# Differential attention in an encoder trunk: the key norms summed by a stationary of ones and inverted on all columns, in place of per-token sums turned back by TensorE

## The chip, the cores and the metric

The kernel runs on one core of one Trainium2 chip. The metric is the device time of one execution in microseconds (us), the median of several. The engines are named as the profile names them: PE (TensorE), DVE (VectorE), ACT (ScalarE), POOL (GpSimd) and SP (SyncE, which issues DMAs).

## The reference

A trunk of two layers over 16 + 512 and 16 + 256 tokens (800 in all), width 1024, all in fp32. Layer 0 mixes with a bidirectional mLSTM, layer 1 with differential attention, and each is followed by a SwiGLU feed-forward layer. The change touches only the attention of layer 1:

```python
def _rms_f32(x, g):
    xf = x.astype(jnp.float32)
    y = xf * lax.rsqrt(jnp.mean(xf * xf, axis=-1, keepdims=True) + RMS_EPS)
    return y * g.astype(jnp.float32)

    q = proj[..., :D_QK_W].reshape(B, L, D_HEADS, 2, D_HD)
    k = proj[..., D_QK_W:2 * D_QK_W].reshape(B, L, D_HEADS, 2, D_HD)
    v = proj[..., 2 * D_QK_W:].reshape(B, L, D_HEADS, 2 * D_HD).astype(jnp.float32)
    q = partial_rope(_rms_f32(q, g_q), cos, sin) * (D_HD ** -0.5)
    k = partial_rope(_rms_f32(k, g_k), cos, sin)
    ...
        s = jnp.einsum("bhcqd,bhckd->bhcqk", qblk, k)
        p = jax.nn.softmax(s, axis=-1)
        a = p[:, :, 0] - lam * p[:, :, 1]
        return jnp.einsum("bhqk,bhkv->bhqv", a, v)
    ...
    o = _rms_f32(o, g_sub) * (1.0 - lambda_init)
```

There are 8 heads, each with two components of 64 rows. Keys need one norm factor per token and component, queries likewise, and the output of each head one per token.

## The kernel before

**Layout.** Activations lie feature by token: a head's keys are one tile of 128 rows (two components of 64) by 800 tokens, its queries 128 by 768 (the 16 learned tokens of each sequence ask nothing). A projection block is 8 steps over the width, `run_block`; a step is 6 matmuls (high and low parts of a split fp32 product, two stretches of tokens). The finished block lies in PSUM banks 6 and 7 until DVE evacuates it (`evacuate`, `evacuate_inner`), and only then may PE open the next block there (`acc_free`).

**The schedule.** Every engine has its own program, written out by hand in one order, and they meet at semaphores. `head(hd, ...)` on each engine attends with head hd and, woven between, projects keys, queries and values of head hd + 1. Query tiles are numbered 0 to 5; tiles 0 to 3 see 528 keys, tiles 4 and 5 see 272. For each tile i: PE computes the scores (`attn_scores`), DVE takes the maxima (`maxima`), ACT the exponentials (`exps`), DVE joins the two components (`combine`), PE turns the result (`turn_attention`), ACT copies it (`turned`), PE multiplies by the values (`attend`), and DVE scales (`output`). Scores of 528 keys fill PSUM banks 0 to 3, so the scores of a tile wait for the exponentials of the tile before. The last scores in `head(hd)` are already those of head hd + 1, tile 0, and so need that head's normalised keys (`kn_ready`). Head 0 and the loop's six heads contain this hand-over, seven in all; head 7 has none.

**Key norms before.** ACT squares the keys (`k_sq`). PE sums them over 64 rows by eight small matmuls: the squares of 128 tokens are the stationary operand and two columns of ones and zeros the moving one (`square_sum`, line 1214), which leaves the sums with tokens on the partitions, 2 columns a tile. ACT takes the roots of all 28 columns (`key_query_roots`), DVE inverts 16 of them and spreads each over 64 columns (`invert_key_roots`), PE turns eight tiles of it back to feature by token (`turn_key_roots`, line 1244), in two parts, and DVE multiplies the keys by what PE left in PSUM (`normalise_k`), in two parts. Query norms stay with tokens on the partitions and are used as scales of the exponentials.

**Output norms before.** The output of head hd - 1 is finished in `head(hd)`: ACT takes roots (`output_roots`), DVE inverts 6 columns and scales six 128 by 128 tiles (`scale_output`, line 2105), PE turns them (`turn_output`, two parts), and ACT and DVE split them (`deliver`).

**Ahead of head 0** the same steps run for head 0's keys, and DVE's order there is: rope of keys and queries, key norms, query norms, then the evacuation of the values block, for which PE's next block waits.

## Time and profile before

| | |
|---|---|
| Time, median of 3 runs | 1863.31 us (1863.25 to 1863.38) |
| Span of the profiled execution | 1860.4 us |
| PE busy (matmuls) | 1849.7 us, 99% |
| DVE busy | 1235.1 us, 66% |
| ACT busy | 879.7 us, 47% |
| POOL busy | 1162.6 us, 62% |
| PE's share of the chain that ended last | 91% |
| Granted clock of PE | 9 (tenths, 9 or more) in all 40 slices |
| Attention layer, head 0 to head 7 | about 943 to 1320 us of the span |

The profiled execution is read by its span; the timed runs are 2.9 us longer than it, since they hold what lies around it. Busy time is the time in which an engine had an instruction under way; for PE the ends of matmuls are modelled and overlap the next, so the distance from start to start is the better price. In the timeline, rows of like instructions are merged, "x6" counting them; an fp32 matmul shows as two records. What stands in brackets is the idle time before the row and what ended it.

### The profile page before, as it was taken

Reading aid. Unit: us, or ns where it says so; the run is one execution under the profiler, and the core shown is the slowest. Engines: PE = TensorE matmul, PEld = TensorE weight load, DVE = VectorE, ACT = ScalarE, POOL = GpSimd, SP = SyncE. Lnnn points to the kernel's source line nnn. Section 1 sums busy time; section 2 is a strip of 40 time slices with the busy share of each in tenths; the row PEclk is TensorE's granted clock in tenths of the full one; section 3 lists DMA queues with packets and bytes.
Section 4 is the critical chain, followed back from the end, with each engine's and each line's share of the span. In section 5 each row is a group of like instructions: output and inputs, shape, how many; then the busy total and the mean of one; then the engine's idle time right before and its main releaser. Section 6 shows DMA issues by size and latency. Waiting matters only on the chain.

```text
span 1860.4 us, 31456 instructions
## 1 busy us (share of the span) xinstructions
PE 1849.7 (99%) x10845; PEld 1742.0 (94%) x10845; DVE 1235.1 (66%) x2072; ACT 879.7 (47%) x1855; POOL 1162.6 (62%) x1533
## 2 busy tenths in 40 slices
PE   9999999999999999999999999999999999999999
PEld 8888889999999999999988888888889999999998
DVE  6756566768576757576876666666587575756663
ACT  6444343455444445454444444444465454444553
POOL 4453644468687878788843333333558788887885
PEclk9999999999999999999999999999999999999999
DMA  8789997549697977774475666664233535353534
GB/s 270 257 240 237 222 259 173 183 108 228 209 237 238 235 227 218 250 232 118 107 145 121 126 124 124 130 118 91 74 90 110 148 99 157 100 153 101 154 112 133
DMA packets 380153, 309.51 MB, mean 166 GB/s; under 512 B 14395, under 2 KB 322398, under 8 KB 379766
## 3 DMA queue, kind: packets, MB, share of 16 engines
q1 hardware_dynamic: 349472, 237.81, 42.1%
q0 software_dynamic: 28416, 69.21, 20.5%
q8 instruction: 73, 1.20, 0.3%
q10 hardware_dynamic: 2134, 0.82, 0.2%
q14 instruction: 58, 0.48, 0.1%
HBM read 302.16 MB, written 144.04 MB: 240 GB/s over the span
## 4 chain that ended last, share of the span: by engine, by line
PE 91%; DVE 5%; ACT 1%; issue 1%; DMA 1%; POOL 0%; SPq 0%; ACTq 0%; DVEq 0%; POOLq 0%
PE ps L974 51%; PE ps L884 26%; PE ps L1155 3%; PE ps L1312 3%; PE ps L1280 2%; PE ps L1302 1%; PE ps L1130 1%; PE ps L1214 1%; DVE rstd L1502 1%; PE ps L1164 1%; DVE sx L1554 0%; PE ps L1244 0%; DVE mx L2077 0%; DVE gt L1661 0%; DMA wk<-in_x_prompt_dram 0%
## 5 line engine op out<-in xcount | busy, mean ns | idle before, releaser
L974 PE MATMUL ps<-sx,wh 128*128 128x400 f32 (+1 forms) x2044 | 530.3, 340 | 0.9 <-POOL wl L808 0.5
L808 POOL TENSOR_TENSOR wl<-raw,wh 128x256 fp32r<-128x256 f32 (+1 forms) x432 | 355.6, 855 | 97.9 <-ACT wh L2243 96.4
L774 POOL CAST wh<-raw 128x256 fp32r<-128x256 f32 x248 | 102.5, 456 | 450.6 <-PE ps L884 424.9
L974 PEld LDWEIGHTS ps<-sx,wh 128*128 128x128 f32 x2044 | 373.4, 188 | 3.0 <-ACT gt_first L2258 0.9
L974 PE MATMUL ps<-sx,wl 128*128 128x400 f32 (+1 forms) x1022 | 347.6, 340 | 0.0
L808 POOL TENSOR_TENSOR wl<-raws,wh 128x256 fp32r<-128x256 f32 x328 | 283.8, 910 | 84.4 <-ACT wh L2243 84.0
L1715 DVE TENSOR_TENSOR h<-h,ps 128x400 f32<-128x400 f32 (+1 forms) x280 | 154.5, 559 | 131.5 <-PE ps L974 131.4
L974 PE MATMUL ps<-fx,wh 128*128 128x400 f32 (+1 forms) x904 | 235.3, 341 | 0.1
L884 PE MATMUL ps<-xh,wh 128*128 128x512 f32 (+1 forms) x752 | 211.2, 357 | 0.0
L884 PE MATMUL ps<-xl,wh 128*128 128x512 f32 (+1 forms) x752 | 207.3, 349 | 0.0
L778 POOL TENSOR_TENSOR wl<-raw,wh 128x256 fp32r<-128x256 f32 x248 | 198.8, 831 | 5.1
L884 PE MATMUL ps<-xh,wl 128*128 128x512 f32 (+1 forms) x752 | 201.3, 345 | 0.0
L2243 ACT ACTIVATE wh<-raw 128x512 fp32r<-128x512 f32 (+2 forms) x268 | 142.7, 535 | 106.5 <-PE ps L974 92.3
L974 PEld LDWEIGHTS ps<-sx,wl 128*128 128x128 f32 x1022 | 191.9, 188 | 0.0
L2243 ACT ACTIVATE wh<-raws 128x512 fp32r<-128x512 f32 (+2 forms) x202 | 108.5, 538 | 159.0 <-PE ps L974 150.5
L974 PEld LDWEIGHTS ps<-fx,wh 128*128 128x128 f32 x904 | 164.6, 188 | 0.5 <-issue 0.5
L974 PE MATMUL ps<-fx,wl 128*128 128x400 f32 (+1 forms) x452 | 153.7, 340 | 0.0
L974 PE MATMUL ps<-sx,w5h 128*128 128x400 f32 (+1 forms) x532 | 138.3, 341 | 0.3 <-ACT gt L2258 0.3
L884 PEld LDWEIGHTS ps<-xl,wh 128*128 128x128 f32 x752 | 126.2, 188 | 10.2
L884 PEld LDWEIGHTS ps<-xh,wl 128*128 128x128 f32 x752 | 124.5, 188 | 10.8
L884 PEld LDWEIGHTS ps<-xh,wh 128*128 128x128 f32 x752 | 120.6, 189 | 14.5 <-issue 3.8
L808 POOL TENSOR_TENSOR w5l<-raw,w5h 128x256 fp32r<-128x256 f32 x112 | 94.8, 868 | 22.5 <-ACT w5h L2243 22.1
(330 smaller groups left out, 3552.0 us busy)
## 6 DMA issues: line engine op xcount, KB each, us to landing
in_sums<-in_ffn_w_in_dram SPq DMA_DIRECT2D x16, 1536.0 KB, 10.7
raw<-in_sums SPq DMA_DIRECT2D x96, 256.0 KB, 3.0
in_sums<-in_ffn_w_in_dram SPq DMA_DIRECT2D x16, 1280.0 KB, 7.2
raw<-in_ffn_w_in_dram SPq DMA_DIRECT2D x80, 256.0 KB, 3.0
raws<-in_sums SPq DMA_DIRECT2D x80, 256.0 KB, 3.1
raw<-out_sums SPq DMA_DIRECT2D x120, 128.0 KB, 2.6
raws<-in_ffn_w_in_dram SPq DMA_DIRECT2D x52, 256.0 KB, 3.1
raw<-in_m_w_in_dram SPq DMA_DIRECT2D x24, 512.0 KB, 4.8
```

Source lines behind the costliest of these rows:

```text
L774: ins = pool.tensor_copy(wh[:, slot, c], raw[:, slot, c])
L778: ins = pool.tensor_tensor(wl[:, slot, c], raw[:, slot, c], wh[:, slot, c].bitcast(F32), ALU.subtract)
L808: ins = pool.tensor_tensor(slot_of(n, 1)[:, c], raw_of(n)[:, c], slot_of(n, 0)[:, c].bitcast(F32), ALU.subtract)
L884: mm = pe.matmul(out, w[:, slot, k * P:(k + 1) * P], x[:, k, a:b], start=(k + q == 0), stop=(k == k_tiles - 1 and q == 2), skip_group_chec ...
L974: mm = pe.matmul(product_bank(layer, s, j), slot_of(n, low_w)[:, k * P:(k + 1) * P], x, start=(j in OPENS and k + q == 0), stop=(k == tile ...
L1130: mm = pe.matmul(flat(2)[0:tz, base + a:base + a + columns], k[:, 1, t0:t0 + tz], q[:, 0, START[s] + a:START[s] + a + columns], start=(t = ...
L1155: mm = pe.matmul(ps[0:tz, state_bank(i) + d, 0:M_DV + 2], w, v, start=(j == js[0] and t == 0), stop=(j == js[-1] and t == len(passes) - 1) ...
L1164: mm = pe.transpose(flat(2)[:, c * 1024 + t0:c * 1024 + t0 + tz], hn(i)[0:tz, c * P:(c + 1) * P], ident[0:tz, 0:tz])
L1280: return pe.matmul(both[:, c, a:b], wk[rows, odd, i * P:(i + 1) * P], wk[rows, 2 + odd, START[s] + a:START[s] + b], start=True, stop=True)
L1312: mm = pe.matmul(acc_o, at[:, i % 2, q, :], va[:, odd, j, :], start=(q == 0), stop=(j == js[-1]), skip_group_check=True)
L1715: ve.tensor_tensor(part, part, product_bank(layer, s, j), ALU.add if result_of(s, j)[0] >= 4 else ALU.subtract).then_inc(out_read, 1)
L2243: sc.activation(slot_of(n, 0)[:, 0:columns], raw_of(n)[:, 0:columns], ACT.Copy).then_inc(prod_hi, 1)
```

## The change

Key squares are summed by two matmuls whose stationary operand is a 128 by 128 matrix with two 64 by 64 blocks of ones (`blocks`), and whose moving operand is the 800 columns of squares, 512 and 288. The sums then lie feature by token already, each repeated over the 64 rows of its component. ACT takes the roots of all 800 columns, DVE inverts all 800 in SBUF, and multiplies the keys by them in one instruction. `turn_key_roots` and the spreading copy are gone. The scaling of the outputs goes to ACT, with the reciprocal left on DVE (the last two heads keep it on DVE). On PE the scores of the next head's tile 0 and the first part of `turn_output` move behind step 5 of the values block and `attend(4)`; one step earlier a wait for `o_ready` moves from `turn_attention` to `attend` for tiles 4 and 5. Ahead of head 0, its first scores move behind the first step of head 1's keys block.

```diff
             def key_sums(g, k, done=None):
...
-                keys = [lambda i=i: square_sum(i) for i in range(NQ, NQ + NT)]
-                return {k: [squares] + keys[0:4], k + 1: keys[4:]}
+                    pe.matmul(bank[:, 0:K_PART], blocks, k_sq[:, 0:K_PART], start=True, stop=True, skip_group_check=True)
+
+                def second():
+                    pe.matmul(ps[:, 0, 0:T - K_PART], blocks, k_sq[:, K_PART:T], start=True, stop=True,
+                              skip_group_check=True).then_inc(ks_done, 1)
+
+                return {k: [first], k + 1: [second]}
...
                 if first:
-                    keys_block(0, 3)
+                    keys_block(0, 1)
+                    attn_scores(0, 0, 0, first=True)
+                    keys_block(1, 3)
...
                 attend(hd, odd, 3)
-                if not last:
-                    turn_key_roots(hd + 1, 0)
-                beside(values_block, 3, 4, (2, 4, 5))
-                if not last:
-                    turn_key_roots(hd + 1, 1)
-                beside(values_block, 4, 5, (2, 5, 6))
+                beside(values_block, 3, 5, (2, 4, 6))
                 turn_attention(hd, 4, first)
 
-                if not last:
-                    attn_scores(hd + 1, even, 0)
-                if not first:
+                if last:
                     turn_output(hd - 1, even, 0)
                 beside(values_block, 5, 6, (3, 0, 3))
                 attend(hd, odd, 4)
+                if not last:
+                    attn_scores(hd + 1, even, 0)
+                    if not first:
+                        turn_output(hd - 1, even, 0)
+                    values_block(6, 8)
                 if not first:
                     turn_output(hd - 1, even, 1)
...
+            def invert_output_roots(hd):
+                ve.wait_ge(oroot, hd + 1)
+                ve.reciprocal(rs[:, 0:NQ], rs[:, 0:NQ]).then_inc(rs_ready, 1)
+
+            def invert_key_roots(g, part):
                 ve.wait_ge(qk_root, g + 1)
-                v(ve.reciprocal(qkr[:, odd, 2 * NQ:], qk2[:, 2 * NQ:]))
-                v.wait()
-                ve.tensor_copy(key_roots.rearrange("p (i f) -> p i f", i=2 * NT),
-                               qkr[:, odd, 2 * NQ:].unsqueeze(2).to_broadcast([P, 2 * NT, D_HD])).then_inc(lt_ready, 1)
+                columns = (slice(0, K_PART), slice(K_PART, T))[part]
+                v(ve.reciprocal(k_sq[:, columns], k_sq[:, columns]))
...
+            def normalise_k(g, odd, x):
                 v.wait()
-                v(ve.tensor_tensor(kd[rows, odd, at_col], bank[rows, keys.start - a:keys.stop - a], x[rows, keys], ALU.mult))
+                for rows, keys, at_col in ((slice(D_HD, P), slice(0, TAIL), slice(TAIL, 2 * TAIL)),
+                                           (slice(0, D_HD), slice(512, LENS[0]), slice(0, TAIL))):
+                    v(ve.tensor_tensor(kd[rows, odd, at_col], k_sq[rows, keys], x[rows, keys], ALU.mult))
                 v.wait()
-                ve.tensor_tensor(x[:, a:b], bank[:, 0:b - a], x[:, a:b], ALU.mult)\
-                  .then_inc((kn_part, kn_ready)[part], 1)
+                ve.tensor_tensor(x, k_sq, x, ALU.mult).then_inc(kn_ready, 1)
...
                 maxima(hd, odd, 5)
                 if not last:
-                    normalise_k(hd + 1, even, kx, 0)
+                    if not first:
+                        invert_output_roots(hd - 1)
+                    invert_key_roots(hd + 1, 0)
                 output(hd, odd, 3)
-                if not last:
-                    invert_query_roots(hd + 1, even)
-                    normalise_k(hd + 1, even, kx, 1)
-                if not first:
+                if last:
                     scale_output(hd - 1, even)
-
-                if last:
                     add_tile(OUT1 + 2, EARLY[2], 3)
                 else:
+                    invert_key_roots(hd + 1, 1)
+                    normalise_k(hd + 1, even, kx)
+                    invert_query_roots(hd + 1, even)
                     maxima(hd + 1, even, 0)
...
             def key_query_roots(g, bank=turn_bank):
                 sc.wait_ge(ks_done, g + 1)
                 sc.activation(k_sq[:, 0:K_PART], bank[:, 0:K_PART], ACT.Sqrt, bias=epsc, scale=1.0 / D_HD)
                 sc.wait_ge(qks_done, g + 1)
...
+                sc.activation(k_sq[:, K_PART:T], ps[:, 0, 0:T - K_PART], ACT.Sqrt, bias=epsc, scale=1.0 / D_HD)
+                sc.activation(qk2[:, :], square_sums, ACT.Sqrt, bias=epsc, scale=1.0 / D_HD).then_inc(qk_root, 1)
...
+            def scale_output(hd, odd):
+
+                sc.wait_ge(rs_ready, hd + 1)
+                sc.wait_ge(o_ready, hd * NQ + NQ)
+                for i in range(NQ):
+                    ins = sc.activation(on(odd, i), on(odd, i), ACT.Copy, scale=rs[:, i:i + 1])
+                ins.then_inc(os_ready, 1)
```

DVE's program at the end of a head in the loop, from the join of tile 4 (the first row) to the maxima of the next head's tile 0. Before (`spare` is the spread key roots, `ps` what PE turned, `wk` the keys):

```order
L2091 SCALAR_TENSOR_TENSOR wk<-wk,ratio 128x272
L2049 REGISTER_ALU
L2050 RECIPROCAL qkr<-qk 128x16
L251 REGISTER_ALU
L2052 COPY spare<-qkr 128x1024
L2076 REGISTER_ALU
L2077 TENSOR_REDUCE mx<-ps 128x2
L251 REGISTER_ALU
L2079 SCALAR_TENSOR_TENSOR nb<-mx,qkr 128x2
L2070 TENSOR_TENSOR kd<-ps,wk 64x16
L251 REGISTER_ALU
L2072 TENSOR_TENSOR wk<-ps,wk 128x512
```

In the changed kernel the same place, from the maxima of tile 5 on, where `spare` is now the squares, then the roots, then the inverted roots of all 800 columns:

```order
L2070 TENSOR_REDUCE mx<-ps 128x2
L251 REGISTER_ALU
L2072 SCALAR_TENSOR_TENSOR nb<-mx,qkr 128x2
L2046 RECIPROCAL rs<-rs 128x6
L2049 REGISTER_ALU
L2051 RECIPROCAL spare<-spare 128x512
L2089 TENSOR_SCALAR wk<-ps,rsum 128x128
L2051 RECIPROCAL spare<-spare 128x288
L251 REGISTER_ALU
L2064 TENSOR_TENSOR kd<-spare,wk 64x16 x2
L251 REGISTER_ALU
L2066 TENSOR_TENSOR wk<-spare,wk 128x800
```

The reciprocal of 16 columns and the copy stood ahead of the maxima of tile 5; two reciprocals of 512 and 288 columns stand behind it, and all of the keys' multiplication behind those.

PE's program in the same stretch before, from the second part of the turned key roots (L1244): a step of the values block (L884), tile 4 turned (L1302), the next head's tile 0 scores (L1285, L1280), the output turned (L1265):

```order
L1244 MATMUL ps<-cst,spare 128x16 x2
L884 MATMUL ps<-xh,wh 128x400 x2
L884 MATMUL ps<-xl,wh 128x400 x2
L884 MATMUL ps<-xh,wl 128x400 x2
L1298 REGISTER_ALU
L1302 MATMUL ps<-cst,wk 128x128 x2
L1302 MATMUL ps<-cst,wk 16x128
L1275 REGISTER_ALU
L1285 MATMUL ps<-kd,wk 128x2x16
L1280 MATMUL ps<-wk 128x512 x2
L1265 MATMUL ps<-cst,wk 128x128 x4
```

In the changed kernel, from tile 4 turned (L1294) on, `attend` being L1306 and the scores L1277 and L1272:

```order
L1294 MATMUL ps<-cst,wk 128x128 x2
L1294 MATMUL ps<-cst,wk 16x128
L886 MATMUL ps<-xh,wh 128x400 x2
L886 MATMUL ps<-xl,wh 128x400 x2
L886 MATMUL ps<-xh,wl 128x400 x2
L1306 MATMUL ps<-va,at 128x128 x3
L1265 REGISTER_ALU
L1267 REGISTER_ALU
L1277 MATMUL ps<-kd,wk 128x2x16
L1272 MATMUL ps<-wk 128x512 x2
L1257 MATMUL ps<-cst,wk 128x128 x4
```

One step of the block and the attend of tile 4 now stand ahead of the scores, and behind them only the last two steps of the block.

DVE's program ahead of head 0, before, from the end of the queries' rope to the evacuation of the values block (L1478), which PE's next keys block waits for:

```order
L2046 TENSOR_TENSOR wk<-wk,spare 128x768
L2050 RECIPROCAL qkr<-qk 128x16
L2052 COPY spare<-qkr 128x1024
L2070 TENSOR_TENSOR kd<-ps,wk 64x16
L2072 TENSOR_TENSOR wk<-ps,wk 128x512
L2070 TENSOR_TENSOR kd<-ps,wk 64x16
L2072 TENSOR_TENSOR wk<-ps,wk 128x288
L2057 RECIPROCAL qkr<-qk 128x12
L2059 TENSOR_SCALAR qkr<-qkr 128x12
L1478 TENSOR_TENSOR spare<-ps,rstd 128x800
```

And in the changed kernel:

```order
L2042 TENSOR_TENSOR wk<-wk,spare 128x768
L2051 RECIPROCAL spare<-spare 128x512
L2051 RECIPROCAL spare<-spare 128x288
L2064 TENSOR_TENSOR kd<-spare,wk 64x16 x2
L2066 TENSOR_TENSOR wk<-spare,wk 128x800
L2055 RECIPROCAL qkr<-qk 128x12
L2057 TENSOR_SCALAR qkr<-qkr 128x12
L1471 TENSOR_TENSOR spare<-ps,rstd 128x800
```

The order of the three jobs is the same; the first has other instructions, and the evacuation stands behind all of them.

## Rows read from the trace of the kernel before

**Rows 1.** One head by engine: length, busy times, granted clock, DMA share, GB/s

```profile
...
1077.90:1126.30 48.40, 48.30 (x306) 41.52 (x306) 32.45 (x72) 22.12 (x60) 17.26 (x27) 1.00 0.60 119
```

**Rows 2.** PE timeline, head's end into the next: start, us, line, tiles, count

```profile
...
1120.94 0.66 PE L1244 MATMUL ps<-cst,spare 128*128 128x128 f32 x4
...
1124.83 0.31 PE L1285 MATMUL ps<-kd,wk 128*128 128x32 f32 x2
...
1126.12 0.66 PE L1265 MATMUL ps<-cst,wk 128*128 128x128 f32 x4
...
1127.71 0.83 PE L1312 MATMUL ps<-va,at 128*128 128x128 f32 x6
...
1128.85 0.61 PE L884 MATMUL ps<-xh,wh 128*128 128x400 f32 x2
...
1131.45 0.31 PE L1285 MATMUL ps<-kd,wk 128*128 128x32 f32 x2
...
1132.75 0.94 PE L1312 MATMUL ps<-va,at 128*128 128x128 f32 x6
1133.44 0.61 PE L884 MATMUL ps<-xh,wh 128*128 128x400 f32 x2
...
1135.71 0.60 PE L1255 MATMUL ps<-cst,spare 128*128 128x128 f32 x4
```

**Rows 3.** DVE timeline beside it; in brackets idle before, releaser

```profile
...
1119.92 0.24 DVE L2050 RECIPROCAL qkr<-qk 128x16 f32<-128x16 f32 x1
...
1120.81 0.71 DVE L2077 TENSOR_REDUCE mx<-ps 128x2 f32<-128x544 f32 x1
...
1121.75 0.18 DVE L2070 TENSOR_TENSOR kd<-ps,wk 64x16 f32<-64x16 f32 x1
...
1122.57 0.34 DVE L2096 TENSOR_SCALAR wk<-ps,rsum 128x128 f32<-128x128 f32 x1
...
1126.24 1.26 DVE L2077 TENSOR_REDUCE mx<-ps 128x2 f32<-128x1056 f32 x1 [0.70 <-PE ps L1280]
...
1128.96 0.50 DVE L2091 SCALAR_TENSOR_TENSOR wk<-wk,ratio 128x272 f32<-128x272 f32 x1
...
1131.33 0.99 DVE L1478 TENSOR_TENSOR spare<-ps,rstd 128x800 f32<-128x800 f32 x1 [0.16 <-PE ps L884]
```

**Rows 4.** PE timeline earlier in that head

```profile
...
1097.74 0.59 PE L884 MATMUL ps<-xh,wh 128*128 128x512 f32 x2
...
1099.91 0.71 PE L1302 MATMUL ps<-cst,wk 128*128 128x128 f32 x5
...
1107.64 0.60 PE L884 MATMUL ps<-xh,wh 128*128 128x512 f32 x2
...
1111.82 0.73 PE L1280 MATMUL ps<-wk 64*128 64x272 f32 x4
```

**Rows 5.** PE timeline ahead of the attention layer: f32 matmuls with ones

```profile
...
914.41 1.50 PE L899 MATMUL ps<-wk,ones 128*128 128x400 f32 x4
...
916.10 0.52 PE L884 MATMUL ps<-xl,wh 128*128 128x512 f32 x2
```

**Rows 6.** One line, reciprocal of 800 columns: ns min, median, max

```profile
...
L1502 DVE RECIPROCAL rstd<-rstd x3: 5142/5153/5153, 413.6 to 1383.1; 128x800 f32<-128x800 f32 x3
```

**Rows 7.** Timeline of ACT beside it

```profile
...
1118.07 0.60 ACT L2665 ACTIVATE at<-ps 128x512 f32<-128x512 f32 x1 [0.23 <-PE ps L1302]
```

**Rows 8.** Timeline of DVE ahead of the first head

```profile
...
934.48 0.25 DVE L2050 RECIPROCAL qkr<-qk 128x16 f32<-128x16 f32 x1
...
938.04 0.99 DVE L1478 TENSOR_TENSOR spare<-ps,rstd 128x800 f32<-128x800 f32 x1
```

**Rows 9.** Timeline of PE at the same place

```profile
...
935.51 1.09 PE L1244 MATMUL ps<-cst,spare 128*128 128x128 f32 x8 [0.27 <-DVE spare L2052]
...
937.74 0.40 PE L1285 MATMUL ps<-kd,wk 128*128 128x32 f32 x2
...
942.81 0.41 PE L1285 MATMUL ps<-kd,wk 128*128 128x32 f32 x2
```

More of the change, by code:

```diff
@@ L83 @@
 A_PER = 72
-ATTN_SET = 9
+ATTN_SET = 11
 NPROD = 7
@@ L467, in trunk @@
         X_COLUMN = (0, 1, 2, 3, 5, 6, 4)
-        key_roots = spare[:, 0, 6:8, :].rearrange("p a b -> p (a b)")[:, 0:NT * P]
         PROBS = 4 * T
@@ L1219, in key_sums, with first @@
             def key_sums(g, k, done=None):
-                def squares():
+                bank = ps[:, 1, :] if done is None else turn_bank
+                def first():
                     pe.wait_ge(qsq_ready, g * 2 + 1)
@@ L1294, in turn_attention @@
             def turn_attention(hd, i, first):
-                if not (first and i == 0):
+                if i < 4 and not (first and i == 0):
                     pe.wait_ge(o_ready, hd * NQ + i)
@@ L2022, in _ @@
             ffn(0)
-            ve.memset(qk2[:, :], 1.0).then_inc(attn_set, 1)
+            ve.memset(blocks, 0.0).then_inc(attn_set, 1)
+            ve.wait_ge(attn_set, ATTN_SET - 2)
+            for rows in (slice(0, D_HD), slice(D_HD, P)):
+                ve.memset(blocks[rows, rows], 1.0).then_inc(attn_set, 1)
             ve.wait_ge(attn_set, ATTN_SET)
@@ L2055, in invert_query_roots @@
             def invert_query_roots(g, odd):
                 ve.wait_ge(qk_root, g + 1)
-                v(ve.reciprocal(qkr[:, odd, 0:2 * NQ], qk2[:, 0:2 * NQ]))
+                v(ve.reciprocal(qkr[:, odd, :], qk2[:, :]))
                 v.wait()
-                v(ve.tensor_scalar(qkr[:, odd, 0:2 * NQ], qkr[:, odd, 0:2 * NQ], D_HD ** -0.5, None, ALU.mult))
+                v(ve.tensor_scalar(qkr[:, odd, :], qkr[:, odd, :], D_HD ** -0.5, None, ALU.mult))
                 v.wait()
-            def normalise_k(g, odd, x, part, bank=turn_bank):
-                a, b = ((0, TILES[4][1]), (TILES[4][1], T))[part]
-                rows, keys, at_col = ((slice(D_HD, P), slice(0, TAIL), slice(TAIL, 2 * TAIL)),
-                                      (slice(0, D_HD), slice(512, LENS[0]), slice(0, TAIL)))[part]
-                ve.wait_ge(lt_turned, g * 2 + (part + 1))
+            def normalise_k(g, odd, x):
@@ L2193, in _ @@
             rope_end(0, qx, 0)
-            invert_key_roots(0, 0)
-            normalise_k(0, 0, kx, 0)
-            normalise_k(0, 0, kx, 1, second_bank)
+            for part in range(2):
+                invert_key_roots(0, part)
+            normalise_k(0, 0, kx)
             invert_query_roots(0, 0)
@@ L2715, in head @@
                 exps(hd, odd, 5)
+                turned(hd, 4)
                 squared(hd, odd, 3)
-                turned(hd, 4)
+                if not first and not last:
+                    scale_output(hd - 1, even)
                 if not first:
```

59 lines of the change are left out of this document (20 added, 39 removed).

## The prediction, made before the changed kernel ran

> **What bounds the kernel now.** I read the page first: PE is busy for 1849.7 of 1860.4 us and makes up 91% of the chain that ended last, so only what shortens PE's program, or makes it wait, moves the time. Then the stretches: in one attention head PE is busy for 48.30 of 48.40 us at a full granted clock, DVE for 32.45 [rows 1]. A busy engine whose ends are modelled can hide small waits, so I went to the timelines of PE and DVE at the end of a head. That stretch is one head, 48.4 us; the next one's own scores begin at 1131.45 [rows 2]. The reader is to see there that PE runs without a gap, and that DVE, though idle for a third of the head, is not idle at its end: from 1119.92 to the maxima at 1126.24 it has 0.70 us of idle time [rows 3]. The next head's scores start at 1124.83 [rows 2], and need keys that DVE finishes between 1122.57 and then. That hand-over is what the change rebuilds.
>
> **What PE is spared.** Two steps of a queries block take 1099.91 - 1097.74 = 2.17 us; the two that carry the eight key sums take 1111.82 - 1107.64 = 4.18 [rows 4]. The sums cost 2.01. Their successors are full fp32 matmuls of 800 columns. The nearest row is the same shape, ones as the stationary operand, 800 columns in four records: to 1.69 us from its start the block behind has also run a pair that costs 2.17 / 6 = 0.36, so it costs 1.33 [rows 5]. Spared: 0.68. The eight transposes go: 1120.94 to 1124.83 is 3.89 us [rows 2] and becomes two steps of 400 + 400 columns, 1135.71 - 1133.44 = 2.27, and the turning of tile 4. That turning is what 1128.85 to 1131.45 holds beside two steps: 2.60 - 2.27 = 0.33 [rows 2]. So 3.89 becomes 2.60, spared 1.29, waits included. Together 1.97 us a head, in seven heads.
>
> **What the keys now wait for.** DVE's work up to 1119.92 follows the queries block and is continuous, so it too comes 0.68 earlier: 1119.24. In a row behind it, with prices start to start: maxima of tile 5, 1121.75 - 1120.81 = 0.94 [rows 3]; reciprocal of 6 columns, 0.2 (that of 16 has 0.24 [rows 3]); two reciprocals; output 3, 0.34 less 0.08 of overlap = 0.26 [rows 3]; two small products of 0.18 with gaps, 0.4 [rows 3]; the product of 800 columns, 0.99 (evacuations of 800 columns are two-input instructions of the same size [rows 3, 8]). The reciprocal of 800 columns takes 5.15 us [rows 6], 21 times the 0.24 of 16 columns: (5.15 - 0.24) / 784 = 6.3 ns a column. Hence 512 columns take 3.35 and 288 take 1.95, with overlap 5.25 together. Sum: 0.94 + 0.2 + 5.25 + 0.26 + 0.4 + 0.99 = 8.04, keys ready at 1127.3.
>
> The Trainium skill ("VectorE: DVE Perf Modes", First, the fixed hardware budget) says that the reciprocal is an iterative divide with a repeat count of 8. Taken as 8 cycles a column at the page's 0.96 GHz that would be, as an estimate, 6.7 us for 800 columns; the trace has 5.15, and the measurement decides. By the page each hand-over would be 1.4 us later still.
>
> **When PE asks for them.** Before at 1124.83. Now 1.97 earlier, but with one step (1.14) and attend 4 (1133.44 - 1132.75 = 0.69 [rows 2]) moved ahead: 1124.69. So PE waits 1127.33 - 1124.69 = 2.6 us, and the scores start 2.50 later than before, although 1.97 of PE's work is gone and 1.83 was moved out of their way.
>
> **What is late next.** All that DVE does behind the maxima of tile 0 moves by 2.5 us too. PE behind the scores: 1.29 for them (1126.12 - 1124.83), 0.45 for the first outputs turned (1.59 to 1127.71 less a step), two steps 2.27, second part 0.2: it asks for the join of tile 5 at 1131.54. DVE ended that join at 1129.46 [rows 3]; 2.5 later, less 0.15 of idle time that closes, is 1131.8. Wait 0.3, then 0.33: the next head starts at 1132.19, 0.74 later than 1131.45. The evacuation of the values ended at 1132.32 [rows 3] and now ends between 1134.2 and 1134.8; PE asks for the bank at 1133.44 + 0.74 = 1134.18. That is a wait of 0 to 0.7, I take 0.35; and 0.1 (0 to 0.3) for ACT's copy of the values, which hangs on the same chain. A head becomes 0.74 + 0.35 + 0.1 = **1.2 us longer**, seven times 8.4 (0.7 to 1.6 a head: 5 to 11).
>
> **ACT.** Two roots of 512 and 288 columns come ahead of the copy for attend 3. ACT starts that copy, itself a read of 512 columns of PSUM, at 1118.07 after 0.23 of waiting, and it takes 0.60 [rows 7]. At 0.60 each at most, the roots add 1.2, less 0.68: the copy is up to 0.5 late. Attend 3 has five tiles, 1.15 at the rate of attend 4, so it began at about 1120.94 - 1.15 = 1119.8 [rows 2] and had some 0.9 to spare. So no wait; if a root costs double, 0.3 a head. The six scalings moved to ACT begin behind output 3, at about 1124.4, and at 0.6 each at most end by 1128.0, before PE turns them at 1127.3 + 1.3. On DVE they stood behind the keys and ahead of an idle 0.70 [rows 3]: nothing is won there.
>
> **Ahead of head 0** nothing covers the reciprocals. DVE's rope ends at 934.48 [rows 8]; three small clears in place of one, 0.25 (0.1 to 0.4). Then 5.25 + 0.4 + 0.95 (0.99 less overlap), and query norms, two instructions of 12 columns, 0.45: the evacuation starts at 941.8 in place of 938.04 [rows 8] and ends at 942.8. Only then may PE open the keys block; one step 1.14, and the first scores start at 943.95 in place of 937.74 [rows 9]. From there to the second scores exponentials decide (942.81 - 937.74 = 5.07 [rows 9], PE's own work 1.29 + 2.27 = 3.6), before as after, so **6.2 us** (5.5 to 6.7) pass to the end. PE idles for some 7 us in there, where it now has 0.27 [rows 9].
>
> The granted clock is 1.00 throughout [rows 1], and no row has PE idle for microseconds and busy behind it. Below, the clock stays: 0. Above, it falls to the lower level, 1.2 of 2.4 GHz, and the step and the scores on the path (1.14 + 1.29) take twice as long: 2.4, and 3.2 with the two steps that follow, 4.5 then against 3.8 of exponentials. I take 1.2, as no row decides.
>
> The Trainium skill ("TensorE: Matmul & The Clock Gate", What's actually happening) says that the clock falls to its lower level when PE has been idle and rises after sustained work. By that rule the term is 2.4 to 3.2 and the time 1.2 to 2 us above mine; by the rows alone it could be 0.
>
> **Sum** against the profile's own 1860.4: 6.2 + 8.4 + 1.2 = 15.8, that is 1876.2 as a span, and with the 2.9 around it 1879.1 against the median of 1863.3. I say 1879.
>
> **Rivals.**
> (1) *PE is spared and nothing waits.* DVE's reciprocals would have to be hidden. Then seven times -1.97, and ahead of head 0 -0.68 and -1.36 for the transposes and their wait [rows 9]: 1847.5. For it: DVE is idle for a third of a head, and 0.24 us for 16 columns looks cheap. Against it: [rows 6]. Each us off the pair of reciprocals takes 1 us off every one of eight places, so the sign turns where the pair costs 14.6 / 8 = 1.8 us less, 3.4 in place of 5.25. Chance 0.05.
> (2) *A draw*, within 0.2%, which is 3.7 us and about what a measurement tells: the same with the pair at 3.0 to 3.9, or with only the wait ahead of head 0 and hand-overs that break even: 1863 to 1867. Chance 0.04.
> (3) *The clock falls at every hand-over*, not only ahead of head 0. The scores and what follows them, 1.3 to 3 us, would take twice as long in seven heads: 9 to 21 more, 1888 to 1900. Against it: waits of 2.6 us only. Chance 0.06.
> (4) *The waits are smaller, and a loss stays*: some instruction of the DVE chain overlaps more than I count, 0.5 to 1 us a head: 1868 to 1874. Chance 0.15.
> (5) *My forecast*, 1874 to 1884: 0.70.
> Range 1868 to 1887. Faster 0.05, same 0.04, slower 0.91.
>
> **What the changed profile would show.** Reciprocals of 512 and 288 columns at 3.35 and 1.95 us; at each of seven scores of tile 0 PE idle for about 2.6 us, released by DVE's product of 800 columns; heads 49.6 apart in place of 48.4; an idle stretch of 7 us ahead of head 0, released by DVE's evacuation; no L1244; the pair of steps with key sums at 3.5 in place of 4.18; the clock just behind 942.8 shows which end of its term holds. The feed-forward stretches must be unchanged. I am wrong if reciprocals in place on the squares run at another rate than in place on the root of the norm, or if PE's idle time is not in front of these scores.

## The result: slower, and by more than predicted

The changed kernel takes 1890.85 us (median of 4 runs, 1888.74 to 1891.48) against 1863.28 (1862.69 to 1863.38): 1.0146 times, 95% interval 1.0133 to 1.016. That is 27.6 us slower; the prediction had 15.8, and its range ended at 1887. The profiled execution of after took 1891.11 us, its span 1889.1.

**The profile after.** The page, from the busy times and from the chain that ended last; before, PE made up 91% of the chain and DVE 5%:

```profile
PE 1849.7 (98%) x10685; PEld 1733.3 (92%) x10685; DVE 1263.0 (67%) x2030; ACT 894.8 (47%) x1899; POOL 1160.0 (61%) x1533
...
PE 81%; DVE 11%; issue 4%; ACT 3%; DMA 1%; POOL 0%; DVEq 0%; SPq 0%; ACTq 0%; POOLq 0%
```

PE is "busy" for as long as before, although it does less. These are the waits of PE from 930 to 1310 us (total, times, longest), in a program for which the same list held two waits before, of 0.3 and 0.2 us:

```profile
PE ps L1277 <- DVE wk L2066: 15.3, 7, 2.4
PE ps L886 <- DVE spare L1471: 7.4, 2, 7.2
PE ps L1247 <- ACT va L2650: 2.4, 4, 0.8
PE ps L1294 <- DVE wk L2084: 0.9, 3, 0.3
```

The first row is the forecast wait for the keys: six times 2.2 to 2.4 us, and 1.45 in the last. DVE's chain ahead of it, in the head of 1196 us:

```profile
1189.20 3.31 DVE L2051 RECIPROCAL spare<-spare 128x512 f32<-128x512 f32 x1
...
1192.60 1.94 DVE L2051 RECIPROCAL spare<-spare 128x288 f32<-128x288 f32 x1
...
1194.98 0.99 DVE L2066 TENSOR_TENSOR wk<-spare,wk 128x800 f32<-128x800 f32 x1
...
1197.62 1.26 DVE L2070 TENSOR_REDUCE mx<-ps 128x2 f32<-128x1056 f32 x1 [1.30 <-PE ps L1272]
```

3.31 and 1.94 us against 3.35 and 1.95 predicted. Now PE at two such places, one head apart:

```profile
1143.93 0.40 PE L1277 MATMUL ps<-kd,wk 128*128 128x32 f32 x2 [2.33 <-DVE wk L2066]
1144.26 2.08 PE L1272 MATMUL ps<-wk 64*128 64x512 f32 x4
1146.27 1.11 PE L1257 MATMUL ps<-cst,wk 128*128 128x128 f32 x4
...
1196.11 0.40 PE L1277 MATMUL ps<-kd,wk 128*128 128x32 f32 x2 [2.32 <-DVE wk L2066]
1196.44 1.13 PE L1272 MATMUL ps<-wk 64*128 64x512 f32 x4
```

The waits are equal, 2.33 and 2.32 us. Behind the first the scores take 2.08 us, behind the second 1.13. The busy times by stretch say why; the number behind POOL's is the granted clock:

```profile
1141.60:1143.93 2.33, 0.01 (x1) 0.01 (x1) 2.23 (x5) 1.10 (x4) 0.00 (x0) 1.00 0.58 109
1143.93:1145.00 1.07, 1.07 (x4) 0.80 (x6) 0.18 (x2) 0.00 (x0) 0.00 (x0) 0.65 0.00 0
1145.00:1146.00 1.00, 1.00 (x4) 0.00 (x0) 0.00 (x0) 0.00 (x0) 0.00 (x0) 0.50 0.00 0
...
1148.00:1150.00 2.00, 1.98 (x12) 1.70 (x10) 1.38 (x4) 1.83 (x5) 0.04 (x1) 1.00 0.00 0
...
1196.11:1198.11 2.00, 2.00 (x11) 1.20 (x12) 0.67 (x2) 0.00 (x0) 0.00 (x0) 1.00 0.20 37
```

The clock falls to 0.50, the lower of its two levels (1.2 of 2.4 GHz), at four of the seven hand-overs (1041, 1092, 1144 and 1247 us). At the first three it falls once PE works again, for some 3 us. At the fourth it is already down while PE still waits, and stays down for some 7 us (busy times by stretch again):

```profile
1244.40:1246.20 1.80, 0.00 (x1) 0.00 (x0) 1.70 (x4) 1.12 (x4) 0.00 (x0) 1.00 0.95 172
1246.20:1247.00 0.80, 0.24 (x2) 0.24 (x2) 0.74 (x3) 0.00 (x0) 0.00 (x0) 0.78 0.24 44
1247.00:1253.00 6.00, 6.00 (x19) 4.41 (x20) 2.74 (x6) 2.24 (x5) 0.00 (x0) 0.50 0.03 5
```

That head is the longest, 53.0 us. Ahead of head 0 the clock falls too, 2.6 us after PE's wait began:

```profile
936.31 0.53 PE L886 MATMUL ps<-xh,wl 128*128 128x400 f32 x2
944.06 1.03 PE L886 MATMUL ps<-xh,wh 128*128 128x400 f32 x2 [7.23 <-DVE spare L1471]
...
946.23 0.47 PE L1277 MATMUL ps<-kd,wk 128*128 128x32 f32 x2
946.62 2.08 PE L1272 MATMUL ps<-wk 64*128 64x512 f32 x4
...
951.95 0.41 PE L1277 MATMUL ps<-kd,wk 128*128 128x32 f32 x2 [0.40 <-ACT wk L2659]
```

PE is idle for 7.2 us as forecast; the step behind it takes 2.17 us (1.21 at the same place before) and the scores 2.40 (1.38).

**Where the time is.** The second scores of head 0 start at 951.95 (942.81 before [rows 9]); DVE's long reciprocal of rstd ahead of all this already starts 1.1 us later, so 8.0 belong to the change. From there to the start of the last head's own scores (a head's own scores are those of tile 1, the first in its program) pass 352.0 us, 333.5 before: 18.5. Middle heads are 50.8 to 53.0 us long, before 48.4 [rows 1]. The two profiled spans, 1889.1 and 1860.4, are 28.7 us apart; the 2.2 us that are left lie ahead of and behind the attention, where the change has nothing.

### The profile page after: what moved, and what is told of

Its sections match the earlier page's. It is cut to its first block, busy times and chain, and to the rows that moved or that the text cites. A ratio compares the mean times of both kernels' runs of the same rounds, so it can differ in the third digit from the quotient of the medians.

```text
span 1889.1 us, 31124 instructions
## 1 busy us (share of the span) xinstructions
PE 1849.7 (98%) x10685; PEld 1733.3 (92%) x10685; DVE 1263.0 (67%) x2030; ACT 894.8 (47%) x1899; POOL 1160.0 (61%) x1533
## 4 chain that ended last, share of the span: by engine, by line
PE 81%; DVE 11%; issue 4%; ACT 3%; DMA 1%; POOL 0%; DVEq 0%; SPq 0%; ACTq 0%; POOLq 0%
PE ps L976 50%; PE ps L886 21%; PE ps L1157 3%; PE ps L1272 2%; PE ps L1306 1%; DVE spare L2051 1%; DVE mx L2070 1%; PE ps L1132 1%; DVE rstd L1495 1%; PE ps L1294 1%; DVE spare L2033 1%; PE ps L1166 1%; ACT wk L2659 1%; DVE spare L2030 0%; DVE wk L2040 0%
## 5 line engine op out<-in xcount | busy, mean ns | idle before, releaser
L886 PE MATMUL ps<-xh,wh 128*128 128x512 f32 (+1 forms) x752 | 219.0, 366 | 7.7 <-DVE spare L1471 7.4
```

The lines of the kernel that those rows point to most:

```text
L886: mm = pe.matmul(out, w[:, slot, k * P:(k + 1) * P], x[:, k, a:b], start=(k + q == 0), stop=(k == k_tiles - 1 and q == 2), skip_group_chec ...
```

## Experiments

Two questions: is the clock the whole of the missing 12 us, and why does a head lose more than the wait explains? Shown edits are against after unless said otherwise. The kernel before, timed again beside each group of them, had medians of 1862.5 to 1863.0 us.

### PE's idle time filled

```diff
                 attend(hd, odd, 4)
                 if not last:
+                    pe.wait_ge(qk_root, hd + 2)
+                    for _ in range(12):
+                        pe.matmul(turn_bank[:, 0:HT], wh[:, even, 0:P], xh[:, 0, 0:HT], start=True, stop=True, ...)
                     attn_scores(hd + 1, even, 0)
...
             run_block(MIX1 + 2, 0, 3, k0=7)
+            for _ in range(30):
+                pe.matmul(turn_bank[:, 0:P], blocks, ident, start=True, stop=True, ...)
```

> After, with PE's seven waits at the hand-overs filled: twelve spare matmuls of 400 columns into a bank that nobody reads then, about 2.2 us at full clock, stand behind attend 4 and ahead of the next head's first scores. Nothing that the output needs is changed. Theory A (the part of the loss that was not forecast is TensorE's clock, which falls behind the idle time): the granted clock stays at 1.00 behind all seven hand-overs, the scores' row of 64x512 takes 1.13 us in each, the second scores of the heads stand 49.5 to 49.8 us apart rather than 50.8 to 53.0, and the time is 1881 to 1884 us; the 8.45 us ahead of head 0 stay. Rival B (the scores are slowed by something else that runs then, such as VectorE's reciprocals or ScalarE's scalings in the neighbouring banks): the time stays at 1890 us and the rows keep 1.7 to 2.1 us. Rival C (fillers delay the scores more than they save): over 1891.

Measured with the first part alone: 1885.24 us (1884.72 to 1885.75), ratio to before 1.0122 (1.0105 to 1.0139). All seven scores take 1.13 us at a granted clock of 1.00; the PE timeline of one:

```profile
1088.88 2.43 PE L1389 MATMUL ps<-xh,wh 128*128 128x400 f32 x12
1091.46 0.40 PE L1277 MATMUL ps<-kd,wk 128*128 128x32 f32 x2
1091.79 1.13 PE L1272 MATMUL ps<-wk 64*128 64x512 f32 x4
```

> The kernel with filled hand-overs, and thirty more spare matmuls of 128 fp32 columns (6.4 us at full clock) in PE's idle time of 7.2 us ahead of head 0. Theory A: the keys block and the first scores behind it run at a granted clock of 1.00, 1.14 and 1.38 us rather than 2.17 and 2.40, so the second scores start some 2 us earlier: 2 us less than with the hand-overs alone, 1879 to 1882 us, which is the forecast without its clock term. Rival B: no difference to the run with the hand-overs alone. Rival C: the fillers start at a lowered clock, take twice as long and push the keys block out: 2 to 5 us more.

Measured with both: 1883.15 us (1883.02 to 1883.46). The keys block behind the idle time is at full clock again:

```profile
935.81 6.86 PE L1420 MATMUL ps<-cst 128*128 128x128 f32 x60
943.22 0.64 PE L886 MATMUL ps<-xh,wh 128*128 128x400 f32 x2 [0.55 <-DVE spare L1477]
```

**What follows.** A is right in its mechanism and B falls: spare work alone, with no wait shortened, gives back 5.6 and 2.1 us. The clock costs 7.7 us in all, where the forecast had 1.2. But both times lie 1.2 us above A's bands, and middle heads are still 49.8 to 50.8 us long, not the 49.5 to 49.8 that I expected: from the second scores of head 0 to the last head's own pass 347.4 us, 13.9 more than before, where the forecast had 8.4. These 5.5 us are not the clock.

> After, with six spare matmuls ahead of each hand-over's first scores in place of twelve: 1.1 us of the 2.3 us wait are filled at its start, PE is idle for about 1.2 us behind them. Theory A (short idle times are harmless, as the 1.29 us in the run with the inversion hidden): the clock stays up at all seven, 1884 to 1886 us as with twelve. Rival B (any idle time near the scores can bring it down, by chance): the clock falls at one to three hand-overs, 1886 to 1890 us.

Six fillers in place of twelve: 1885.20 us (1884.66 to 1885.73), no fall at any hand-over, with PE idle for 1.1 to 1.3 us ahead of six of them (0.35 in the last). A holds.

### The order of PE's tail undone

Scores of tile 0 and the first turned outputs ahead of the sixth step and attend 4, as before.

> After, with PE's tail in the order of before: the next head's first scores and the first turned outputs stand ahead of the sixth step of the values block and of attend 4 again. Theory A: the keys come at the same time, PE asks 1.8 us earlier and waits 4.1 to 4.5 us in each head, then has 1.8 us more to do behind the scores; with 0.6 of other waits closed that is 1.0 to 1.4 us more in a head, 7 to 10 us, and the clock falls at all seven hand-overs, some 1 to 2 us at three more: 1898 to 1905 us. Rival B (the order makes no difference, since VectorE's chain ends last either way): 1889 to 1892.

Measured: 1900.37 us (1899.65 to 1900.85). PE's waits, 930 to 1310 us:

```profile
PE ps L1277 <- DVE wk L2062: 27.7, 7, 4.1
```

3.9 to 4.1 us each (3.2 in the last), and behind each of the seven the clock falls. As A: given DVE's chain, the new order is right, and worth 9.5 us.

### The inversion left out

```diff
-                v(ve.reciprocal(k_sq[:, columns], k_sq[:, columns]))
+                v(ve.tensor_scalar(k_sq[:, columns], k_sq[:, columns], 1.0, None, ALU.mult))
```

> After, with the two reciprocals of the key roots replaced by multiplications by 1.0 of the same columns in the same place: the inversion of the keys' roots is left out, all waits and orders stand. Theory A (the reciprocals' 5.25 us on VectorE make PE wait, and the wait brings the clock down): a multiplication of 512 columns takes 0.3 to 0.6 us, the pair about 1, so the keys are ready 4.2 us earlier, before PE asks; no wait at the hand-overs, clock 1.00 in all of them, PE's idle time ahead of head 0 at 3 us, and the time is 1848 to 1853 us, faster than before by 0.6 to 0.8%. Rival B (the new order of PE's tail or ScalarE's added work costs time of itself): 1863 us or more, with waits at other places.

Measured: 1862.84 us (1861.59 to 1863.82), ratio 1.0002 (0.9992 to 1.0011). **A falls; B holds** within the noise: it had 1863 or more, with waits at other places. No wait for the keys is left, and the 28 us are gone, but a middle head is 48.0 to 48.2 us long where 46.4 should do. Ahead of head 0 PE still waits 2.27 us, the clock falls there in this profile, and the second scores come 3.0 us later than before. The timelines of DVE, ACT and PE behind the scores of tile 0, which start at 1078.06:

```profile
1079.47 1.26 DVE L2070 TENSOR_REDUCE mx<-ps 128x2 f32<-128x1056 f32 x1 [3.15 <-PE ps L1272]
...
1082.18 0.50 DVE L2084 SCALAR_TENSOR_TENSOR wk<-wk,ratio 128x272 f32<-128x272 f32 x1
...
1082.74 0.55 PE L1294 MATMUL ps<-cst,wk 128*128 128x128 f32 x3 [0.33 <-DVE wk L2084]
...
1090.68 0.59 ACT L2650 ACTIVATE va<-ps 128x512 f32<-128x512 f32 x1
...
1091.32 0.66 PE L1247 MATMUL ps<-cst,spare 128*128 128x128 f32 x4 [0.83 <-ACT va L2650]
```

Read down: DVE's maxima wait for the scores; the join of tile 5 (L2084) stands behind them on DVE and ends 4.62 us after the scores began; PE, which now has only 4.2 us of work behind the scores, waits. What DVE does next (values evacuated, tile 0 joined, maxima of tile 1) is late by the same, ACT's exponentials and then its copy of the values (L2650) behind them. Before, that copy was ready 1.0 us ahead of the matmuls that turn it, the second L1255 of the head whose own scores start at 1131.45 [rows 2]:

```profile
1136.72 0.59 ACT L2650 ACTIVATE va<-ps 128x512 f32<-128x512 f32 x1
...
1138.33 0.60 PE L1255 MATMUL ps<-cst,spare 128*128 128x128 f32 x4
```

It began 5.27 us after the head's own scores; here it is 7.42 (1090.68 against 1083.26), 2.15 more. Laid beside before from own scores to own scores, the gaps are 0.56 at the join, 0.17 at the values' bank, 0.95 at the second half of the turned values: 1.7 us a head. The same three stand in the kernel with all idle time filled. None of it needs the reciprocals; it needs scores of tile 0 that stand 5.2 us ahead of the head's own, 6.6 before [rows 2].

### The same, with the old order, and then with VectorE's scaling

> The kernel without the inversion (multiplications by 1.0 in place of the two reciprocals; the inversion of the keys' roots is left out), with PE's tail back in the order of before: first scores ahead of the sixth step of the values block and of attend 4. The last run left 14 us unexplained: without the reciprocals PE never waits for the keys, yet a head is 48.06 us long and not 46.4. Theory A (the new place of the first scores costs it: they stand 5.2 us ahead of the head's own scores in place of 6.6, and VectorE's maxima, the join of tile 5, the evacuation of the values and ScalarE's copy behind them all hang on those scores; gaps of 0.56, 0.17 and 0.99 us follow): with the old order the gaps close, a head takes 46.4 to 46.7 us, and the time is 1850 to 1854 us. Rival B (ScalarE's two wide roots and six scalings, which stay, are what makes the copies late): a head stays at 48.0, the time at 1861 to 1864.

Measured: 1861.67 us (1860.6 to 1863.65), middle heads of 48.03 to 48.09. A named the right gaps, they are gone, and the time is not. B has the time and, in the scalings, the cause, though not by way of the copies. ACT's and PE's timelines:

```profile
1122.96 1.84 ACT L2639 ACTIVATE wk<-wk,rs 128x128 f32<-128x128 f32 x6
...
1124.86 0.66 PE L1257 MATMUL ps<-cst,wk 128*128 128x128 f32 x4 [1.46 <-ACT wk L2639]
```

The scaling that the change gave to ScalarE ends 2.8 us after the scores began at 1122.04, and in the old order PE wants to turn the scaled outputs 1.3 us after the scores began. So it goes back to VectorE:

```diff
                     invert_query_roots(hd + 1, even)
+                    if not first:
+                        scale_output(hd - 1, even)
                     maxima(hd + 1, even, 0)
```

> The kernel without the inversion and with the old order of PE's tail, and now with the scaling of the outputs back on VectorE, behind the keys and ahead of the next maxima, as before the change (the inversion of the keys' roots is left out). The run with ScalarE's scalings showed that the order alone gives nothing: the gaps at the join, the values' bank and the values' copy were gone, but PE waited 1.5 us in each of six heads for ScalarE's scaling when it came to turn the outputs, and a head stayed at 48.0 us. Theory A (the two things that the change did to PE's tail belong together: ScalarE's scalings end 2.8 us after the old place of the scores, so they force the late place, and the late place delays the chain behind the scores): with VectorE scaling, all waits are gone, a head takes 46.4 to 46.7 us, time 1849 to 1852 us, which is what PE is spared. Rival B (a further wait of the same size comes up behind this one): 1857 to 1862.

Measured: 1853.41 us (1853.14 to 1854.19), ratio 0.9948 (0.9931 to 0.9964); every middle head 46.76 to 46.80 us. Of the waits inside a head above 0.2 us in total this is left (925 to 1320 us):

```profile
PE ps L1257 <- DVE wk L2094: 1.4, 6, 0.2
```

A holds: what PE is spared comes out only with neither of the two other parts of the change. The time is 1.4 us above A's band, which had left out the 2.9 us that PE still idles ahead of head 0; the second scores there start 1.8 us later than before (944.62).

> After, whole, with only the scaling of the outputs back on VectorE (behind the keys, ahead of the next maxima; the reciprocal of six roots with it). Theory A: in the late order the scalings are off the path on either engine, as VectorE waits 1.30 us for the first scores there; the 0.16 us of the six roots' reciprocal goes from ahead of the keys, so the keys come 0.1 us earlier: 1889 to 1892 us, the same waits of 2.2 to 2.3 us. Rival B (ScalarE's 1.85 us of scalings are what makes the copy of the values late): the waits for that copy go, 5 to 6 us less: 1884 to 1886.

Measured in after itself: 1889.79 us (1889.38 to 1891.38), waits of 2.2 to 2.3 us, clock fallen at two of seven. As A: there the time does not tell the two engines apart, though PE now waits 0.3 us for VectorE's scalings in five hand-overs. ScalarE's scaling costs time only together with an early turn.

### The reciprocals hidden, or given to another engine

> After, with every inverse root of the attention computed on ScalarE as Exp(-0.5 * Ln(x)) in place of Sqrt there and a reciprocal on VectorE; PE's order as after. ScalarE gets an Exp of 800 columns more (0.9 to 1.2 us in a head) and, if Ln and Exp share a table, loses two table loads of 1.28 us. Theory A (the reciprocals' time on VectorE is the cause of the waits for the keys, the order of PE's tail of 1.7 us a head besides): as without the inversion, no wait for the keys, heads of 48.0 us, 1860 to 1864 us. Rival B (Ln and Exp lie in different tables: 1.28 us at each change, four or more a head on ScalarE, copies late): 1870 to 1890.

Measured: 1907.12 us (1905.77 to 1907.82); with PE's old order 1905.00 (1902.19 to 1905.74):

> The kernel with Exp(-0.5 * Ln(x)) on ScalarE, and PE's order as before in two places: the first scores ahead of the sixth step and of attend 4 in each head, and ahead of the keys block in head 0. Theory A: both causes are gone, a head takes 46.4 to 46.8 us against 48.37 before, the first scores of head 0 come at 937.5 to 938.5 us; seven times 1.6 to 1.9 less: 1849 to 1853 us, faster than both kernels. Rival B: the copies of ScalarE, now with the roots' second function ahead of them, come late for attend 3, 0.5 to 1 us a head: 1854 to 1860.

B of the first is right, and its price was set too low; both theories of the second missed. ACT's groups by line in the first kernel (count, total, mean ns, idle before):

```profile
L2611 ACT ACT_TABLE_LOAD x8 | 10.3, 1283 | 0.1
L2616 ACT ACT_TABLE_LOAD x8 | 10.3, 1283 | 0.1
```

Its PE's waits, 925 to 1320 us:

```profile
PE ps L1306 <- ACT at L2654: 28.6, 7, 4.6
```

Ln (L2611) and Exp (L2616) load a table of 1.28 us each, as do the two functions of the outputs' roots. All that stands ahead of the copy for attend 3, and PE waits for it seven times, 4.2 to 4.6 us in six of them. In these six the clock falls as well, in both kernels. So these runs do not test what a free inverse root on ScalarE would give.

Then the reciprocal of 512 columns was moved into DVE's idle time ahead of the queries' evacuation, with key sums and ACT's key roots earlier and PE's tail in the old order:

```diff
-                beside(queries_block, 2, 6, (1, 3, 6))
+                beside(queries_block, 2, 6, (1, 3, 6), weave=key_sums(hd + 1, 4, hd * (2 * NQ) + 8))
                 turn_attention(hd, 2, first)
 
-                beside(queries_block, 6, 8, None, weave=key_sums(hd + 1, 6, hd * (2 * NQ) + 8))
+                beside(queries_block, 6, 8, None)
...
                 squared(hd, odd, 1)
+                if not last:
+                    key_roots(hd + 1)
...
                 combine(hd, 3)
+                    invert_key_roots(hd + 1, 0)
                     evacuate_inner(n + 1, 3, qx, False)
```

> After, with the whole computation kept and four things moved: the key sums two steps earlier in the queries block, ScalarE's roots of the keys right behind them, VectorE's reciprocal of the first 512 columns into its idle time of 4.5 us ahead of the queries' evacuation, and PE's tail in the order of before. ScalarE loads its table of roots once more in each head, 2 x 1.28 us. Theory A (what counts is where the 5.25 us lie, not that they exist): 3.3 of them are hidden, the keys are ready at 46.4 less 4.6 in the head, some 0.9 us after PE asks; a head takes 47.2 to 47.6 us, no clock falls at the hand-overs, and only the loss of 8.5 us ahead of head 0 stays: 1863 to 1867 us. Rival B (the reciprocals slow VectorE wherever they stand, since its chain from the queries' evacuation on starts later): 1870 or more.

Measured: 1869.53 us (1869.16 to 1871.52), ratio 1.0038 (1.0024 to 1.0053), between the two theories. DVE's timeline:

```profile
1115.62 3.35 DVE L2047 RECIPROCAL spare<-spare 128x512 f32<-128x512 f32 x1 [1.23 <-ACT spare L2626]
1118.92 1.02 DVE L1482 TENSOR_TENSOR wk<-ps,rstd 128x512 f32<-128x512 f32 x2
```

PE's waits, 925 to 1320 us:

```profile
PE ps L1277 <- DVE wk L2062: 9.0, 7, 1.3
```

The same 3.35 us now lie in a gap of DVE, and the time is 21.3 us less than after's, although the order of PE's tail, which cost after 9.5 us, is the old one. The wait is 1.29 us a head (A said 0.9, since the reciprocal pushes the evacuation back by 0.3), the clock stays up, and a head takes 48.1 (A said 47.2 to 47.6).

> The kernel with the first 512 columns inverted in VectorE's idle time, whole computation, ScalarE scaling, with the first scores one step later than in the old order: behind the sixth step, ahead of attend 4. Theory A: in the old order PE waited 1.29 us for the keys in each head; one step is 1.14 us, so 0.1 to 0.2 of it stays; ScalarE's scalings (ready 42.6 us into the head) are asked for at 42.6; the join of tile 5 is asked for 4.9 us after the scores, where it takes 4.7. A head takes 46.6 to 47.0 us, seven times 1.1 to 1.4 less than 48.1: 1860 to 1862 us, the gain of the heads just pays for the 8 us ahead of head 0. Rival B (the chain behind the scores becomes late by what PE no longer waits, as it did without the inversion): a head stays near 48, 1868 to 1870.

Measured: 1869.49 us (1868.22 to 1874.35), middle heads still 48.03 to 48.17: B's time. In this order, the mid order, the wait for the keys is 0.2 us and another has its place, at the second part of the turned outputs (PE's waits, 925 to 1320 us):

```profile
PE ps L1257 <- DVE yl L2105: 7.7, 6, 1.6
```

> That kernel, and ahead of head 0 the inverse roots of the keys by ScalarE, which is idle there, as Exp(-0.5 * Ln(x)) in place of VectorE's reciprocals of 5.15 us (one table load of 1.28 us between the two functions), with the first scores ahead of the keys block again. Theory A: the keys are ready at 938.0 to 938.5 us where before had 937.7 and after 946.2, the second scores start at 943 to 944; 7 to 8 us less than with the mid order alone: 1852 to 1854 us, faster than before by 0.5 to 0.6%. Rival B (the clock falls behind PE's idle time of 1.5 us there, as it did behind 1.84 us in the kernel with ScalarE's inverse roots): 1 to 2 us more.

Measured: 1860.57 us (1860.14 to 1864.97), ratio 0.9989 (0.9979 to 0.9998). Head 0's loss is gone (first scores at 938.75, second at 943.96, clock up), as A said, and with it 8.9 us. Heads stay at 48.03; A's time was reckoned from the 1860 to 1862 us that the mid order had not given.

> The last kernel (512 columns inverted in VectorE's idle time, head 0 by ScalarE, first scores one step later than in the old order), with one thing undone more: the outputs are scaled by VectorE again, behind the keys and ahead of the next maxima. The last run showed why: a head stayed at 48.0 us although the keys were only 0.2 us late, because PE waited 1.2 us for VectorE's product that clears the bank for the second part of the turned outputs, which hangs on the first part, on ScalarE's scalings. Theory A: that wait goes, 0.2 to 0.3 us for the keys and 0.2 for the scaling stay, a head takes 46.9 to 47.3 us, seven times 0.75 to 1.1 less: 1852 to 1855.5 us, faster than both kernels. Rival B (VectorE's six scalings, now ahead of the maxima of tile 0, make the chain behind them late again): 1858 to 1861.

Measured: 1863.00 us (1861.88 to 1863.76), outside both bands. Heads take 48.45, 0.4 more than in the last kernel, for VectorE's scaling now stands ahead of the turn. A falls: the wait of 1.20 us stands as it was, so it does not hang on ScalarE's scalings. PE's, ACT's and DVE's timelines of one hand-over show what the heads wait for:

```profile
1029.51 0.66 PE L1257 MATMUL ps<-cst,wk 128*128 128x128 f32 x4 [0.33 <-DVE wk L2095]
1030.00 0.83 PE L1306 MATMUL ps<-va,at 128*128 128x128 f32 x6
...
1030.37 0.69 ACT L2676 ACTIVATE yh<-ps,gsub 128x512 f32 x1 [3.09 <-PE ps L1257]
...
1031.23 0.75 DVE L2104 SCALAR_TENSOR_TENSOR yl<-ps,gsub,yh 128x512 f32 x1 [0.42 <-ACT yh L2676]
...
1032.04 0.44 PE L1257 MATMUL ps<-cst,wk 128*128 128x128 f32 x2 [1.20 <-DVE yl L2104]
```

The two halves of the turned outputs share a bank; between them ACT copies and DVE multiplies, and the second half starts 2.0 us after the first is through. The mid order had left one attend (L1306, some 0.7 us start to start) in between. So the second half now stands behind one more step of the values block (`values_block(6, 7)`), and the outputs are scaled by ScalarE again:

> The kernel with 512 columns inverted in idle time, head 0 by ScalarE, ScalarE's scalings and the first scores one step later (1860.6 us), with one more line moved: the second part of the turned outputs stands one step of the values block later. Theory A (the wait of 1.20 us there is the chain of turned part, ScalarE's copy of 0.69 and VectorE's product of 0.75, which the old order covered with a step of 1.14 and attend 4 and the mid order with attend 4 alone): the wait falls to 0.1 us, the product for the values' evacuation is not late, a head takes 46.9 to 47.3 us in place of 48.03, seven times 0.75 to 1.1: 1853 to 1855.5 us, faster than before by 0.4 to 0.5%. Rival B (the time comes back at the values' bank and at the copy of the values): 1858 to 1861.

Measured: **1857.20 us** (1856.26 to 1858.83), ratio 0.9968 (0.9955 to 0.998): faster than before by 0.3%. Middle heads take 47.55 us, where A said 46.9 to 47.3, and the time lies 1.7 us above A's band and 0.8 below B's: the wait for the turned half is gone, but 0.35 us for the values' copy came back in six heads, as B said. Among the kernels here that compute the whole it is the only one clearly faster than before.

## Why the prediction was wrong

**Right:** the sign, and the mechanism with its places. PE spared: in the kernel without inversion, with old order and VectorE's scaling, a head is 46.77 with 0.24 of wait in it, so 1.84 spared (1.97 predicted). Reciprocals 3.31 + 1.94 (3.35 + 1.95); the row of 5.15 us for 800 columns [rows 6] decided well against the estimate from a repeat count. Wait for the keys 2.2 to 2.4 listed (2.6). PE idle for 7.2 us ahead of head 0 (some 7). ScalarE's roots made nothing late; the pair of steps with key sums took 3.6 (3.5). Two sums of the prediction are 0.05 us off, 1127.33 for 1127.28 and 1132.19 for 1132.14, and change nothing.

**Wrong, in order of size,** against 15.8 us:
- *The head's own length, 13.9 us in place of 8.4 over the seven; in middle heads some 2.3 in place of 1.2.* The step that failed is the last term of a head: "and 0.1 (0 to 0.3) for ACT's copy of the values, which hangs on the same chain". It measured 0.95, and makes up most of the 1.1 that a middle head lacks. I gave it without following the chain. By my own numbers DVE's evacuation of the values would end 2.0 to 2.6 us after the head's own scores, in place of 0.9, so everything behind it (maxima, exponentials, copy) came at least 1.1 us nearer to the work that needs it. The rows show 2.15 us for the copy, and it had 1.0 to spare. The join was also too small, 0.3 for 0.56 measured: I let 0.15 us of DVE's idle time close, but DVE's maxima wait for the scores as before, and the join ends 4.62 us after the scores began, as it did (4.63). The bank was too large, 0.35 for 0.17, and PE was spared 0.13 less. That the late place of the scores is the cause is shown by the kernel without the inversion and with the old order, where these three gaps are closed.
- *The clock at the hand-overs.* Rival 3, with "waits of 2.6 us only" against it and a chance of 0.06. It fell in four of seven: 352.0 against 347.4 us with the idle time filled, 4.6 us in the profiled execution, 5.6 in the medians. The loss lies below the 9 to 21 us of the rival, which had counted all seven heads. The rows of before could not show it, since PE never idled for microseconds there; that was a reason for a larger chance, not a smaller one.
- *The clock ahead of head 0.* Term 1.2 of a range 0 to 3.2. With the idle time filled the second scores start at 949.04 and rstd's reciprocal 0.3 later than before, so 6.0 us are left of the 8.0 (6.2 predicted), and the clock cost 2.1. The Trainium skill ("TensorE: Matmul & The Clock Gate", What's actually happening) says that an idle PE loses its clock; the estimate from it was 2.4 to 3.2, and the trace agrees with the fall and stays just under that.

5.5 + 4.6 + 0.9 - 0.2 are 10.8 of the 11.8 us missing from the medians. The last 1.0 is not accounted for; the profiles also differ by 2.2 us ahead of and behind the attention, where both kernels do the same. Rival 1 was priced at 1847.5 us for hidden reciprocals. The run without them gave 1862.84: even with the cause of the waits taken away, the change as written would have been a draw. Its sums and transposes give some 13 us in seven heads (1.84 each); the heads together are only 3.7 us shorter than before (329.8 against 333.5), the rest goes to the three gaps behind the late scores, and 3.0 us are lost ahead of head 0.

## What to carry to other kernels

An order is two distances: moving work ahead of a producer hides the wait for its inputs, and shortens the time that its own consumers have. Follow the chain behind the moved instruction until it meets the path again, on every engine. When a run without the suspected cost does not reach the time that the sum says, look at the list of waits again before believing either; here three moves in turn only renamed the wait, and each was found by one row. A wait on TensorE has a second price, in the clock behind it, and a few spare matmuls tell the two apart.

## What was not expected of the hardware

- Waits of about 2 to 3 us brought TensorE's granted clock down in some places and not in others. Behind 2.2 to 2.4 us for the keys it fell in four of six hand-overs of after and in two of six of the kernel that differs only in the scaling, with equal waits in both outcomes. Ahead of head 0 it fell behind 1.84 us (ScalarE's inverse roots, old order) and 2.27 us (inversion left out), and not behind 2.24 and 2.87 us in the two other kernels without the inversion; behind 3.15 us (ScalarE's inverse roots) it fell 1.8 us after PE had begun to work again.
- Behind longer waits, 3.2 to 4.1 us in the kernel with the old order and 4.2 to 4.6 us in the two with ScalarE's inverse roots, it fell in all nineteen. In none of the thirteen waits of 1.1 to 1.3 us of two kernels did it fall. So for waits of 2 to 3 us the length alone does not decide it. What else does stays open.
- Three of the four falls at hand-overs of after made their head 0.9 to 1.1 us longer than in the kernel with filled waits, and the clock was up again some 4 us after PE had resumed; the fourth, which began during the wait, cost 2.4 us.
- ScalarE's Ln and Exp, one behind the other, cost a table load of 1.28 us each time.
